# First half of the mixer out-projections ahead of the last normalization, norms spread over the units, scores of two units paired

## What is computed

```python
# layers 0 and 1
o = concatenate([rms_norm(o_moba, g_moba_out), rms_norm(o_dsa, g_dsa_out)])   # 512 + 512 columns
y = o @ w_out                                                                # 1024 x 1024
x = x + gt_m * rms_norm(y, g_post_mix)
# layers 2 and 3
y_s5  = y * sigmoid(y @ w_glu + b_glu)          # 512 columns, y after gelu
o     = _rms_norm(o, head_gain)                 # per head of 128
y_gla = o * silu(g_out)                         # 512 columns
y = concatenate([y_s5, y_gla]) @ w_out
x = _layer_norm(ALPHA * x + (1 + gt_m) * y, ...)
```

## Time and profile before

| | us |
|---|---|
| median of 3 runs | 2712.68 (2710.31 to 2712.70) |
| the profiled execution | 2712.49 |
| its span, first to last instruction | 2710.7 |
| TensorE matmul busy | 2535.3 (94%) |
| VectorE busy | 1809.9 (67%) |
| ScalarE busy | 1309.5 (48%) |
| GpSimd busy | 678.7 (25%) |
| mean granted TensorE clock | 0.957 of full |

### The profile page before, as it was taken

One profiled execution on the slowest core, in us unless ns is written; L12 is line 12 of the kernel. 1 busy time (PEld: TensorE's weight loads), 2 busy tenths in 40 slices (PEclk: granted clock), 3 DMA queues, 4 the chain that ended last, 5 costly groups with the idle time before them and its releaser, 6 DMA issues. The chain is left out here.

```text
span 2710.7 us, 37505 instructions
## 1 busy us (share of the span) xinstructions
PE 2535.3 (94%) x14758; PEld 2076.7 (77%) x14758; DVE 1809.9 (67%) x2030; ACT 1309.5 (48%) x1336; POOL 678.7 (25%) x353
## 2 busy tenths in 40 slices
PE   6998999998999978999897699999999999999996
PEld 4875998975998755899674588888887878788884
DVE  1654776664865765755574687777777777777775
ACT  2433543433433122333111476777676767676773
POOL 0000000002910625900360123222332323222223
PEclk9999999998999978999897799999999999999997
DMA  9895864575874655865431399999999999999992
GB/s 338 288 301 180 265 206 152 156 251 171 265 223 145 199 187 171 284 199 171 124 109 57 127 364 331 368 328 367 331 363 331 347 351 348 346 346 352 333 361 103
DMA packets 434956, 693.86 MB, mean 256 GB/s; under 512 B 37690, under 2 KB 255894, under 8 KB 434838
## 3 DMA queue, kind: packets, MB, share of 16 engines
q1 hardware_dynamic: 407632, 677.17, 72.7%
q10 hardware_dynamic: 27206, 15.03, 2.0%
HBM read 691.10 MB, written 1.05 MB: 255 GB/s over the span
## 5 line engine op out<-in xcount | busy, mean ns | idle before, releaser
L1408 ACT ACTIVATE region_part<-ring 128x2048 fp32r<-128x2048 f32 x448 | 835.6, 1907 | 307.1 <-PE bank L822 191.2
L822 PE MATMUL bank<-ring_part,region_part 128*128 128x512 f32 x1648 | 649.7, 394 | 0.0
L2265 DVE TENSOR_TENSOR ring_part<-ring,region_part 128x2048 fp32r<-128x2048 f32 x270 | 640.4, 2405 | 2.8 <-ACT region_part L1408 2.8
L820 PE MATMUL bank<-region_part 128*128 128x512 f32 x1432 | 583.4, 407 | 6.2 <-DVE ring_part L2265 6.2
L821 PE MATMUL bank<-region_part 128*128 128x512 f32 x1296 | 512.7, 396 | 0.0
L1300 POOL TENSOR_TENSOR ring_part<-ring,region_part 128x2048 fp32r<-128x2048 f32 x54 | 268.3, 4977 | 554.8 <-ACT region_part L1408 554.8
L822 PEld LDWEIGHTS bank<-ring_part,region_part 128*128 128x128 f32 x1648 | 310.3, 188 | 71.1
L820 PE MATMUL bank<-xn_part,region_part 128*128 128x256 f32 x1152 | 327.6, 284 | 10.4 <-DVE hT_part L1980 9.1
L820 PEld LDWEIGHTS bank<-region_part 128*128 128x128 f32 x1432 | 270.3, 189 | 75.3 <-issue 14.6
L822 PE MATMUL bank<-hT_part,region_part 128*128 128x256 f32 x1152 | 326.0, 283 | 0.0
L821 PE MATMUL bank<-xn_part,ring_part 128*128 128x256 f32 x1152 | 325.6, 283 | 0.0
(11 more groups left out here) (309 smaller groups left out, 4046.1 us busy)
## 6 DMA issues: line engine op xcount, KB each, us to landing
ring<-in_moe_w_gate SPq DMA_DIRECT2D x126, 1024.0 KB, 5.1
ring<-in_moe_w_up SPq DMA_DIRECT2D x126, 1024.0 KB, 5.2
ring<-in_moe_w_down SPq DMA_DIRECT2D x126, 1024.0 KB, 5.0
ring<-in_w_ada SPq DMA_DIRECT2D x48, 1024.0 KB, 7.2
ring<-in_mod_w SPq DMA_DIRECT2D x48, 1024.0 KB, 5.8
ring<-in_w_in SPq DMA_DIRECT2D x44, 1024.0 KB, 5.7
ring<-in_w_up_act SPq DMA_DIRECT2D x22, 1024.0 KB, 5.4
ring<-in_w_up_lin SPq DMA_DIRECT2D x22, 1024.0 KB, 6.3
```

Source lines behind the costliest of these rows:

```text
L820: nc.tensor.matmul(o, split(a_hi), split(b_hi), start=start, stop=False, skip_group_check=True)
L822: return nc.tensor.matmul(o, split(a_hi), split(b_lo), start=False, stop=stop, skip_group_check=True)
L1408: return nc.scalar.activation(out_, in_, func, **kw).then_inc(*done(*event))
L2265: v.tensor_tensor(split(w), w, whole(hi), ALU.subtract).then_inc(*done("moe_lo", j, e))
```

## The change

- **Scores in pairs.** In the attention loop, even iterations compute the scores of units u and u + 1, product by product in turn and in two banks; odd iterations compute none.
- **Norms one by one.** The norm of each (g, t) output is made separately: ScalarE squares after units 4, 8 and 10 and once behind the loop, VectorE makes the variance after iterations 6, 10 and 12 and scales after 7, 11 and 13; the fourth is made behind the copy of the modulation sum. GpSimd takes four powers of one column instead of one of four.
- **Out-projection by token tile and chunk.** `out_tokens(l, n, t)` does the four products of chunk n for tile t. In layers 0 and 1 the first group's blocks are turned at the end of iteration 12; behind the loop come chunk 0 for both tiles, the transposes of the second group, and chunk 1. In layers 2 and 3 chunk 0 for both tiles and chunk 1 for tile 0 come between the value products and the wait for `gla_o`; chunk 1 for tile 1 comes behind the transposes. `out_second` is what `out_projection` did with chunks 2 and 3.
- **Banks.** The four output tiles have fixed banks 4, 6, 5, 7; the GLA products have banks 2 and 3 and their transposes 0 and 1. In layer 2 the copy of the modulation sum, which frees bank 5, goes ahead of the S5 multiplication.

```diff
@@ -735,7 +735,7 @@
-            if u < len(UNITS1):
+            if u < len(UNITS1) and u % 2 == 0:
@@ -745,13 +745,18 @@
-                s = bank(("sc", l, u), ("att_mask", l, u), range(5))
-                for i, h in enumerate(unit_heads(t, n)):
-                    r = 64 * (h % 2)
-                    m = nc.tensor.matmul(s[:, i * kn:(i + 1) * kn],
-                                         qk[r:r + 64, (1, 0)[g], h // 2, t * P:(t + 1) * P],
-                                         qk[r:r + 64, (2, 3)[g], h // 2, 0:kn], start=True, stop=True)
-                m.then_inc(*done("pe_tile", "sc", l, u))
+                pair = (u, u + 1)
+                tiles = [bank(("sc", l, w), ("att_mask", l, w), range(5)) for w in pair]
+                heads = [unit_heads(t, n), unit_heads(t, n + 1)]
+                for i in range(len(heads[0])):
+                    for w, s, hs in zip(pair, tiles, heads):
+                        h = hs[i]
+                        r = 64 * (h % 2)
+                        m = nc.tensor.matmul(s[:, i * kn:(i + 1) * kn],
+                                             qk[r:r + 64, (1, 0)[g], h // 2, t * P:(t + 1) * P],
+                                             qk[r:r + 64, (2, 3)[g], h // 2, 0:kn], start=True, stop=True)
+                        if i == len(hs) - 1:
+                            m.then_inc(*done("pe_tile", "sc", l, w))
             ada_sum(l + 1, "mix", u, 0)
@@ -783,37 +788,50 @@
-
-    def o_transposes(l):
-        for b in range(4):
-            pe.wait_ge(*until("att_on", l, b // 2, 1))
+            if u == len(UNITS1):
+                o_transposes(l, 0, range(5))
+        pe.wait_ge(*until("oT_out", l, 1))
+        for t in range(NT):
+            out_tokens(l, 0, t)
+        o_transposes(l, 1, range(4))
+        for t in range(NT):
+            out_tokens(l, 1, t)
+        pe.wait_ge(*until("oT_out", l, 3))
+
+    def o_transposes(l, g, among):
+        for t in range(NT):
+            pe.wait_ge(*until("att_on", l, g, t))
+        for b in (2 * g, 2 * g + 1):
             transposes(("oT", l, b), ("oT_out", l, b),
                        [(i * S + t * P, xn[:, t, (2 * b + i) * P:(2 * b + i + 1) * P])
-                        for i in range(2) for t in range(NT)], range(4))
-
-    def out_projection(l):
-
-        tiles = [bank(("y", l, "mix", i), y_free(l, "mix", i), range(4, 8)) for i in range(4)]
-
-        def part(n, ts):
-            w = chunk(("out", l, n))
-            for k in range(2):
-                kk = 2 * n + k
-                for t in ts:
-                    for c in range(2):
-                        m = nc.tensor.matmul(tiles[2 * t + c], hT[:, kk, t * P:(t + 1) * P], w[:, k, c * 512:(c + 1) * 512],
-                                             start=kk == 0, stop=kk == KD - 1, skip_group_check=True)
-            return m
-
-        for n in range(2):
-            pe.wait_ge(*loaded(("out", l, n)))
-            part(n, (0, 1)).then_inc(*done("pe_used", "out", l, n))
-        pe.wait_ge(*loaded(("out", l, 2)))
-        part(2, (0,))
-        pe.wait_ge(*loaded(("out", l, 3)))
-        part(3, (0,)).then_inc(*done("pe_used", "y", l, "mix"))
-        for n in (2, 3):
-            part(n, (1,)).then_inc(*done("pe_used", "out", l, n))
+                        for i in range(2) for t in range(NT)], among)
+
+    y_tiles = [None] * 4
+
+    def out_tokens(l, n, t):
+
+        key = ("out", l, n)
+        pe.wait_ge(*loaded(key))
+        if n == 0:
+            for c in range(2):
+                i = 2 * t + c
+                y_tiles[i] = bank(("y", l, "mix", i), y_free(l, "mix", i), ((4, 6, 5, 7)[i],))
+        w = chunk(key)
+        for k in range(2):
+            kk = 2 * n + k
+            for c in range(2):
+                m = nc.tensor.matmul(y_tiles[2 * t + c], hT[:, kk, t * P:(t + 1) * P], w[:, k, c * 512:(c + 1) * 512],
+                                     start=kk == 0, stop=kk == KD - 1, skip_group_check=True)
+        if t:
+            m.then_inc(*done("pe_used", *key))
+        elif n == 3:
+            m.then_inc(*done("pe_used", "y", l, "mix"))
+
+    def out_second(l):
+
+        for t in range(NT):
+            for n in (2, 3):
+                out_tokens(l, n, t)
@@ -1024,20 +1042,24 @@
-            o = bank(("go", l, t), ("gla_o", l, t))
+            o = bank(("go", l, t), ("gla_o", l, t), (2 + t,))
...
             m.then_inc(*done("pe_tile", "go", l, t))
+        pe.wait_ge(*until("s5_done", l))
+        for t in range(NT):
+            out_tokens(l, 0, t)
+        out_tokens(l, 1, 0)
         pe.wait_ge(*until("gla_o", l, 1))
...
             transposes(("goT", l, b), ("goT_out", l, b),
...
-                        for i in range(2) for t in range(NT)])
+                        for i in range(2) for t in range(NT)], (b,))
+        out_tokens(l, 1, 1)
         pe.wait_ge(*until("goT_out", l, 1))
-        pe.wait_ge(*until("s5_done", l))
@@ -1177,12 +1199,10 @@
             attention(l)
-            o_transposes(l)
-            pe.wait_ge(*until("oT_out", l, 3))
...
-        out_projection(l)
+        out_second(l)
@@ -1369,7 +1389,9 @@
-            power(stat[:, 36:40], l, "o")
+            for g in range(2):
+                for t in range(NT):
+                    power(stat[:, 36 + 2 * g + t:37 + 2 * g + t], l, "o", g, t)
@@ -1543,6 +1565,20 @@
+        def o_squares(g, t):
+            act.wait_ge(*until("att_o", l, g, t))
+            act.wait_ge(*done.prev())
+            run(junk[:, 0:512], xn[:, t, g * 512:(g + 1) * 512], ACT.Square, "o_ssq", l, g, t,
+                accum_out=stat[:, 16 + 2 * g + t:17 + 2 * g + t])
+
+        def o_turned(bs):
+            for b in bs:
+                p_ = tile("oT", l, b)
+                for i in range(2):
+                    k = 2 * b + i
+                    name = ("oT_out", l, b) if i else ("act_chain", l, "oT", b)
+                    run(hT[:, k, :], p_[:, i * S:(i + 1) * S], ACT.Copy, *name, scale=col(l, "g_moba_out", 1, k))
+
@@ -1559,18 +1595,11 @@
                 run(att_p[:, u % 2, i * kn:(i + 1) * kn], att_s[:, u % 2, i * kn:(i + 1) * kn], ACT.Exp, *event,
...
-        for g in range(2):
-            for t in range(NT):
-                act.wait_ge(*until("att_o", l, g, t))
-                act.wait_ge(*done.prev())
-                run(junk[:, 0:512], xn[:, t, g * 512:(g + 1) * 512], ACT.Square, "o_ssq", l, g, t,
-                    accum_out=stat[:, 16 + 2 * g + t:17 + 2 * g + t])
-        for b in range(4):
-            p_ = tile("oT", l, b)
-            for i in range(2):
-                k = 2 * b + i
-                name = ("oT_out", l, b) if i else ("act_chain", l, "oT", b)
-                run(hT[:, k, :], p_[:, i * S:(i + 1) * S], ACT.Copy, *name, scale=col(l, "g_moba_out", 1, k))
+            if u in (4, 8, 10):
+                o_squares(*{4: (0, 0), 8: (0, 1), 10: (1, 0)}[u])
+        o_turned((0, 1))
+        o_squares(1, 1)
+        o_turned((2, 3))
@@ -2052,6 +2081,18 @@
     def attention(l):
...
+
+        def spread(g, t):
+            i = 2 * g + t
+            dve.wait_ge(*until("o_ssq", l, g, t))
+            variance(stat[:, 36 + i:37 + i], stat[:, 16 + i:17 + i], 1.0 / 512, 1e-6, l, "o", g, t)
+
+        def finish(g, t):
+            i = 2 * g + t
+            dve.wait_ge(*until("rstd", l, "o", g, t))
+            o = xn[:, t, g * 512:(g + 1) * 512]
+            v.tensor_scalar(o, o, stat[:, 36 + i:37 + i], None, ALU.mult).then_inc(*done("att_on", l, g, t))
+
@@ -2088,13 +2129,13 @@
                         .then_inc(*done("att_o", l, g, t))
-        dve.wait_ge(*until("o_ssq", l, 1, 1))
-        rstd(stat[:, 36:40], stat[:, 16:20], 1.0 / 512, 1e-6, l, "o")
-        for g in range(2):
-            for t in range(NT):
-                o = xn[:, t, g * 512:(g + 1) * 512]
-                v.tensor_scalar(o, o, stat[:, 36 + 2 * g + t:37 + 2 * g + t], None, ALU.mult).then_inc(*done("att_on", l, g, t))
+            if u in (6, 10, 12):
+                spread(*{6: (0, 0), 10: (0, 1), 12: (1, 0)}[u])
+            if u in (7, 11, 13):
+                finish(*{7: (0, 0), 11: (0, 1), 13: (1, 0)}[u])
         acc_out(l + 1, "mix", ADA_MIX - 1)
+        spread(1, 1)
+        finish(1, 1)
@@ -2569,6 +2610,8 @@
             collect(n)
+        if l == 2:
+            acc_out(3, "mix", ADA_MIX - 1)
...
             dve.wait_ge(*until("s5_sig", l, b))
@@ -2585,8 +2628,6 @@
-        if l == 2:
-            acc_out(3, "mix", ADA_MIX - 1)
...
```

## The result

The changed kernel takes 2665.99 us in the median of 4 runs (2664.28 to 2667.11), the kernel before beside it 2712.69 us (2710.31 to 2712.89, 4 runs): ratio 0.9829, 95% interval 0.9812 to 0.9846. The profiled execution took 2666.25 us with a span of 2664.0; its mean granted clock is 0.963 (before 0.957).

A forecast was written before the change was run, and what follows sets the result against it. The prediction took TensorE, busy 2535.3 of 2710.7 us, as the bound: time leaves only by its waits, lower clock or work done side by side. Pairs 11.7 plus tails 31.3 make 43.0 us: 2712.5 - 43.0 = 2669.5 us, range 2661 to 2684.

The forecast's parts named there:

- Pairs, 11.7 us: Attention loops: two units' scores cost 1.09 instead of 2.12 us, so 11 pairs gain 1.06 us each.
- The exception: Layer 1's first pair: the transpose of unit 0 already waits for ScalarE, so this pair gives nothing.
- The cover of 0.8 us: Attention loop: a pair's last exponential ends 3.71 us from its start, the transpose needs it at 4.48, in time by 0.8.
- Tails, 31.3 us: Attention's last products to out-projection's end: filled waits and full clock gain 6.2, 8.1, 8.4 and 8.6 us in layers 0 to 3.
- the 0.3 us per layer for additional changes of work: Tails of all layers: 0.3 us subtracted from the gain because TensorE changes between kinds of work more often.
- Passing on: Behind the out-projection: the 9.6 us from its second chunk's use to the post norm moves along, neither hidden nor longer.
- The weight stream: Attention loop: weight fetches at 355 GB/s could become the next bound and take everything back, 2712 us; chance 0.02.
- A new wait in the loop: Attention loop: the scores' gain goes into a softmax-chain wait, the tails gain alone, 2681 us; chance 0.11.
- The clock did come back: Answers the rival that out-projections begin at the lower clock and transposes keep their cost, 2682 us; chance 0.12.
- more than forecast: FFN's first products, at the lower clock before, profit as well by some 5 us, 2664 us; chance 0.08.
- the change doesn't do what it says: Tails: norms come late or outlast the 16 products, waits only move, 9.8 us less gain, 2679 us; chance 0.05.
- the slower case: Out-projections: TensorE stays at its lower clock through all 256 products, 110 us more, ending at 2780 us; chance 0.03.

The follow-up runs named there:

- pairs_only: The kernel before with the paired scores alone; norms, transposes and out-projections stay where they were: 2697.87 us, ratio 0.9943.
- cover: The changed kernel with VectorE adding the mask three times instead of once in even units, delaying each pair's first exponentials: 2672.81 us, ratio 0.9854.
- after_again: The changed kernel once more, unaltered, for a second profile and a direct comparison: 2663.57 us, ratio 0.9817.
- norms_only: The kernel before with the norms spread over the units, but scores unpaired and all transposes and the out-projection behind the loop: 2709.72 us, ratio 0.9990.
- warm_fit: The kernel before with additional unused products, 4 ahead of the transposes and 1 behind them in all four layers: 2702.20 us, ratio 0.9963.

## Why the prediction was right

**The bound.** Right: what was taken from TensorE's row, and nothing else, came out of the span (everything else changed by 0.2 us); `pairs_only` passed its gain through a wait behind it.

**Pairs, 11.7 us.** 6.5 + 5.3 = 11.8 us in the loops, by both kernels. The exception was right as well: layer 1's first pair waits 1.36 us where it waited 0.17, and gives nothing. The cover of 0.8 us held; `cover` broke it with 1.4 us more.

**Tails, 31.3 us.** 6.9 + 8.9 + 9.4 + 9.5 = 34.8 us (with unrounded terms). The mechanism was right in all four layers (norm covered, copies covered, clock at 1.00), and each forecast is 0.7 to 1.0 us too low. The term that was mis-sized is the 0.3 us per layer for additional changes of work: eight transposes between out-projection products take 211.48 - 210.61 = 0.87 us, less than the 0.98 that they were given, and 24 + 40 instructions take 10.30 + 17.26 = 27.6, no more than in one row. Nothing was to be paid for the changes of work: 1.2 of the 3.5 us. Cheaper transposes are another 0.1 us per eight, 0.6 in all. And the sum let the out-projection begin when the last value product has ended, as it did behind a wait; in one row it begins 0.16 us before that (203.69 against 203.85), 0.6 us in four tails. The value products of layers 2 and 3, which were in no term, differ by what the clock was when they began; the last 1 us or so was not traced further.

**Passing on.** Right in size: from SyncE's fetch to the post norm's first operation 9.6 us before and 9.5 in `after_again` (218.61 to 228.15). As an argument it was incomplete: this chain is the one that ends last behind an out-projection, so its start (chunk 1's use) matters and the out-projection's end doesn't. The weight stream stayed no bound, though the loop moves 352 GB/s now.

**Rivals.** A new wait in the loop did not come, but lies only about 1 us away. The clock did come back; the kernel that shortens the wait without filling it (`norms_only`) shows that this rival was a real one, since there the lower clock moved into the out-projection. The case "more than forecast" named 2664 us, nearer to the 2666.0 measured than the forecast itself, but for a cause that did not come: the stretches with the FFN's first products gained nothing, and what was gained beyond the forecast lies in the tails. That the change doesn't do what it says, the weight stream, and the slower case all fell: in the changed kernel no out-projection has an instruction at the lower clock.

**Sum.** 43.0 forecast; 46.5 measured in the touched stretches, 46.7 in the span. The changed kernel's two medians, 2665.99 and 2663.57, show the size of the last digits: 1 to 3 us of an execution are the clock in places that nothing here touches. The gap of 3.5 us to the forecast is hardly larger than that; what of it lies in the tails repeats from profile to profile, except for the 1.4 us of layer 2's value products.

## What to carry to other kernels

When one engine's row is the kernel, look for what of its own later work is ready during each wait, and move as much as covers the wait, no more; a wait that is only shortened can hand its gain back to the clock. Pairing products that use half the partitions halves their time, and the price is a deadline: work out one pair, from the start of its scores to the first use of its result. Behind a stage, ask which buffer's release starts the next chain, since that use, and not the end of the stage, may be what the next stage waits for.

## What the runs showed of the hardware

What a wait costs by the clock is not told by the wait alone. Behind the same two waits of 3.99 and 0.93 us, with the same instructions between them, layer 1's out-projection took 29.6 us in the kernel before and 27.7 in `pairs_only`. In layer 0 of the kernel before, the clock stayed at 1.00 through the wait of 3.99 us, fell just behind the start of the transposes, at 213.4, and was back at 216.8, 0.1 us after the last of them had ended. In layer 0 of `pairs_only` it was back at 209.9, while the transposes ran on to 210.2. So it rose where TensorE had done nothing but transposes. The Trainium skill (TensorE: Matmul & The Clock Gate, Part 4: PE-mode transpose) says that full clock doesn't engage for transposes; these traces disagree, and the measurement decides. With 3.45 us of waiting in two parts (`norms_only`, layer 0) the stretch of waits and transposes has 0.91 in the mean, and the out-projection behind it 0.61 in its first 7.5 us.

Added work made the kernel faster: 5 more calls per layer that compute nothing took 9.7 us off (`warm_fit`).

Sixteen paired 64-partition instructions take 1.09 us and eight unpaired ones 1.06, with four heads of 128 columns each. An instruction that uses half of the partitions costs as much as a whole one (eight transposes with all 128 partitions and 128 columns take 0.87 us), and its neighbour on the other half is nearly free. The pairs differ from the old scores in two things, the half of the partitions and the bank, and no run here has one without the other. Other banks in turn are not enough by themselves: the out-projection's products alternate between two banks in every kernel and take 0.43 us each.
